# Recurrence of one layer: decays of the four-position level from products of gates in place of exponentials of sums

## The chip, the cores and the metric

The kernel runs on one core of one Trainium2 chip. The time is the device time of one execution of the whole program in microseconds (us), and the number compared is the median of several executions.

## What is computed

Four layers over 256 positions of width 1024, in float32. Each layer has a token mixer (layers 0 and 3: forgetting attention; layer 1: the HGRN2 recurrence; layer 2: a short convolution) and a mixture of experts, each behind a residual and a layer norm. The change touches layer 1's mixer alone:

```python
def hgrn2(x, w_in, lower_bound, norm_g, w_out):
    q, f_logit, i, g = jnp.split(x @ w_in, ...)
    f = lower_bound + (1.0 - lower_bound) * jax.nn.sigmoid(f_logit)
    log_f = jnp.log(f)
    k = 1.0 - f
    # per chunk, 8 heads of 128 key channels and 128 value channels
    b = jnp.cumsum(gb, axis=-2)
    diff = b[:, :, :, None, :] - b[:, :, None, :, :]
    decay = jnp.exp(jnp.where(causal[:, :, None], diff, -jnp.inf))
    scores = jnp.einsum('bhtk,bhsk,bhtsk->bhts', qb, kb, decay)
    o = jnp.einsum('bhts,bhsv->bhtv', scores, ib) + ...
```

Between a key at position s and a query at position t lies the product of the gates f at s+1 to t, for each of 128 channels.

## The kernel before, in words

**Levels.** The kernel does not form the decay of every pair. It cuts the 128 positions of a half of the tokens (c = 0, 1) into blocks of 2m for m = 64, 32, 16, 8, 4, 2, 1 (`LEVELS`). In a block of level m every key of the first half is multiplied by the gates between it and the block's middle, every query of the second half by the gates from the middle on, and the product of the two gives the scores of all pairs whose smallest common block this is. The tile `qk[:, h % 2, c, level, :]` holds these decayed keys and queries of a head, in two copies by turns. The level CROSS goes from the first 128 positions to the second.

**How the decays of a level are made.** Levels 64 to 4 (`SUMMED = 5` of them) and CROSS are exponentials of sums: PE multiplies the logs of the gates (`fg`, tokens on partitions) by tables of zeros and ones (`spans`), which gives the sums in PSUM (L958, L961 to L963), ScalarE drains three banks with `Exp` into `qk` (L1365 and L1367, in the profile as the helper's line L1220), and then DVE multiplies the query halves (L1758, one instruction a level, and L1760 for CROSS) and GpSimd (POOL) the key halves (L719, L721). Levels 2 and 1 (`TWO`, `ONE`) need no exponential: they are products of one or two gates with q or k, by DVE (L1750, L1751, L1753) and POOL (L713, L714), from `fT`, the gates with channels on partitions.

**A head on each engine.** The loop runs over h = 0 to 9, and in turn h each engine issues, in this order:

- PE: the sums of head h (L958 twice, L961, L962, L963); then for head h-1, behind a wait for DVE's `qd_ready` and POOL's `kd_ready`, the cross scores (L971), and for each half of the tokens three products of 128 columns (L978: levels 8, 4 and 2), one of 64 (L979: level 1) and seven small ones (L984: levels 64 to 16) into one bank; the diagonal (L992); then for head h-2 scores times values (L1005 to L1007). A matmul in float32 shows as two records in the profile.
- ScalarE: the three `Exp` drains of head h, the drain of the cross scores, the squares for the norm (L1379).
- DVE: for head h first L1750, L1751, L1753 (behind `sc` of head h-2), then, when all three drains of h are done, five L1758 and L1760. For head h-1 it picks the scores out of the banks (L1769, three L1773, L1780), for h-2 it gates the result (L1788).
- POOL: L713, L714, then behind the same drains five L719 and L721.

Ahead of the loop PE forms the projections of g and i from seven products of blocks each (L816); DVE makes sums of weights for them (L1606 to L1615) and joins the products (L1628, L1630). Behind the loop come the norm of the heads on POOL (L660) and DVE, transposes (L750), the output projection (L844), and, from the event `oT` on, the loads of expert weights into the five buffers that the recurrence's tiles had occupied.

```python
pe.wait_ge(qd_ready, g + 1)
pe.wait_ge(kd_ready, g + 1)
...
elif KINDS[l] == 1:
...
    sp.wait_ge(*filled(("oT", l, TC - 1, 1)))
```

## Time and profile before

| | us |
|---|---|
| median of 3 runs | 1454.54 (1454.23 to 1456.63) |
| the profiled execution | 1453.64 |
| its span, first to last instruction | 1451.8 |
| PE busy | 1307.7 (90%) |
| DVE busy | 365.1 (25%) |
| ScalarE busy | 305.7 (21%) |
| POOL busy | 96.5 (7%) |
| mean granted clock of PE | 0.988 |

Durations in the profile are those of the one profiled execution. A busy PE is one whose records, with modelled ends, leave no gap; the chain that ended last is followed back from the last instruction to what released each step. Times of day in the text, such as 484.78, are us from the start of the span.

### The profile page before, as it was taken

To read this page: it belongs to the slowest core of one execution; us is meant where nothing else is said; L and a number is where in the kernel's file an instruction comes from. 1 tells how busy PE (TensorE), PEld (TensorE's weight loads), DVE (VectorE), ACT (ScalarE), POOL (GpSimd) and SP (SyncE) were. 2 spreads that over 40 slices of the span, in tenths; PEclk is the share of its full clock that TensorE was granted. 3 is DMA by queue.
4 is the path that set the end of the run, shared out by engine and by line. 5 is a ranking of instruction groups with operands and counts; after the bars stand their busy time and mean duration, and the time that the engine had idled before them with its cause. 6 is when DMAs were issued, how large, how long until landed. Compare 5 with 4: busy or idle time off the path is not lost.

```text
span 1451.8 us, 18373 instructions
## 1 busy us (share of the span) xinstructions
PE 1307.7 (90%) x7662; PEld 735.0 (51%) x7662; DVE 365.1 (25%) x928; ACT 305.7 (21%) x751; POOL 96.5 (7%) x170
## 2 busy tenths in 40 slices
PE   8999988878999999898789999888789999988875
PEld 7855634332564766333328865343328765533421
DVE  1442311102624844101002033111112451311103
ACT  0231322211322322212112002222111251222210
POOL 2221000000000520000000000000001130000000
PEclk9999999999999999999999999999999999999998
DMA  9656699999835019999999937999998355899995
GB/s 327 262 226 285 236 430 427 428 426 415 337 116 206 28 56 421 428 428 427 428 425 366 398 117 277 429 427 426 430 423 364 139 232 232 324 427 427 427 427 228
DMA packets 36773, 481.97 MB, mean 332 GB/s; under 512 B 4416, under 2 KB 4736, under 8 KB 6864
## 3 DMA queue, kind: packets, MB, share of 16 engines
q1 hardware_dynamic: 35424, 478.19, 79.8%
q0 software_dynamic: 1120, 2.09, 0.7%
q8 instruction: 66, 1.08, 0.3%
q10 hardware_dynamic: 144, 0.46, 0.1%
q14 instruction: 19, 0.16, 0.0%
HBM read 479.60 MB, written 1.05 MB: 331 GB/s over the span
## 4 chain that ended last, share of the span: by engine, by line
PE 75%; DMA 13%; DVE 5%; ACT 4%; issue 2%; SPq 0%; POOL 0%; DVEq 0%; POOLq 0%
PE psum L785 15%; DMA memory<-in_units 13%; PE psum L1085 12%; PE psum L816 8%; PE psum L1045 8%; PE psum L844 8%; PE psum L1128 7%; PE psum L1120 7%; ACT memory L1224 2%; PE psum L824 1%; DVE memory L1912 1%; PE psum L750 1%; PE psum L1181 1%; ACT memory L1420 1%; PE psum L917 1%
## 5 line engine op out<-in xcount | busy, mean ns | idle before, releaser
L785 PE MATMUL psum<-memory,ring 128*128 128x256 f32 x1024 | 224.7, 382 | 0.4 <-ACT memory L1224 0.4
L785 PEld LDWEIGHTS psum<-memory,ring 128*128 128x128 f32 x1024 | 195.7, 192 | 28.6 <-issue 1.3
L1128 PE MATMUL psum<-memory 128*128 128x512 f32 x256 | 126.5, 619 | 42.9 <-DVE memory L1912 22.8
L1045 PE MATMUL psum<-memory,x 128*128 128x128 f32 x1024 | 131.0, 281 | 35.0 <-ACT memory L1224 35.0
L1045 PEld LDWEIGHTS psum<-memory,x 128*128 128x128 f32 x1024 | 119.8, 192 | 73.1 <-issue 70.2
L1085 PE MATMUL psum<-ring,memory 128*32 128x512 f32 x1152 | 135.9, 611 | 14.1 <-DMA ring<-in_units 13.9
L1224 ACT ACTIVATE memory<-psum,affine_t 128x128 f32<-128x128 f32 x312 | 117.3, 457 | 137.4 <-PE psum L1045 129.8
L1907 DVE TENSOR_TENSOR memory<-memory,psum 128x256 f32<-128x256 f32 x32 | 13.5, 421 | 459.4 <-ACT memory L1414 459.4
L844 PE MATMUL psum<-ring,memory 128*128 128x512 f32 x256 | 112.4, 594 | 1.4 <-DVE memory L1501 0.9
L1128 PEld LDWEIGHTS psum<-memory 128*128 128x128 f32 x256 | 44.0, 190 | 130.7 <-DVE memory L1912 48.2
L1085 PE MATMUL psum<-memory 128*32 128x512 f32 x896 | 103.0, 600 | 4.0 <-DMA memory<-in_units 3.9
L1220 ACT ACTIVATE memory<-psum 128x512 f32<-128x512 f32 (+2 forms) x85 | 45.5, 544 | 203.3 <-PE psum L816 103.4
L1085 PEld LDWEIGHTS psum<-ring,memory 128*32 128x32 f32 x1152 | 35.2, 112 | 104.2 <-issue 87.2
L816 PE MATMUL psum<-ring,memory 128*128 128x512 f32 x200 | 87.8, 593 | 0.0
L1120 PE MATMUL psum<-memory 128*32 128x512 f32 x640 | 79.6, 610 | 7.4 <-DMA memory<-in_units 7.4
L844 PEld LDWEIGHTS psum<-ring,memory 128*128 128x128 f32 x256 | 47.6, 190 | 57.1 <-issue 54.9
L1414 ACT ACTIVATE memory<-psum 128x256 f32<-128x256 f32 x32 | 12.3, 383 | 304.4 <-PE psum L1085 304.4
L1085 PEld LDWEIGHTS psum<-memory 128*32 128x32 f32 x896 | 26.6, 110 | 74.2 <-issue 68.9
L816 PEld LDWEIGHTS psum<-ring,memory 128*128 128x128 f32 x200 | 37.7, 190 | 45.5 <-issue 44.9
L1912 DVE COPY memory<-psum 128x512 f32<-128x512 f32 x32 | 22.1, 692 | 139.0 <-PE psum L1120 139.0
L1420 ACT ACTIVATE memory<-psum 128x512 f32<-128x512 f32 x32 | 19.1, 597 | 179.7 <-PE psum L1120 179.7
L1120 PE MATMUL psum<-ring,memory 128*32 128x512 f32 x384 | 48.8, 627 | 6.4 <-DMA ring<-in_units 6.4
(222 smaller groups left out, 1149.6 us busy)
## 6 DMA issues: line engine op xcount, KB each, us to landing
ring<-in_units SPq DMA_DIRECT2D x129, 2048.0 KB, 25.3
memory<-in_units SPq DMA_DIRECT2D x88, 2048.0 KB, 25.6
memory<-in_units SPq DMA_DIRECT2D x16, 1024.0 KB, 27.3
ring<-in_units SPq DMA_DIRECT2D x4, 512.0 KB, 10.4
memory<-in_const SPq DMA_DIRECT2D x3, 448.0 KB, 31.3
x<-in_x SPq DMA_DIRECT2D x2, 512.0 KB, 4.0
out<-x SPq DMA_DIRECT2D x2, 512.0 KB, 2.7
memory<-in_tables SPq DMA_DIRECT2D x1, 640.0 KB, 31.0
```

The costliest lines, as they stand in the source:

```text
L750: last = nc.tensor.transpose(bank(key, P, i * P), t, ident)
L785: last = nc.tensor.matmul(bank(key, T, s * T), w[:, 2 * m + s, k, :], xT[:, k, :], start=(k == 0), stop=(k == KD - 1))
L816: last = nc.tensor.matmul(bank(key), tokens[:, k, :], weights[:, k, :], start=(k == 0 and p not in (6, 7, 3)), stop=(k == KD // 2 - 1), sk ...
L844: last = nc.tensor.matmul(psum[:, 4 + NH * c + h, :], lhs[:, k, c * P:(c + 1) * P], w[:, k, :], start=False, stop=(k == KD - 1), skip_grou ...
L1045: last = nc.tensor.matmul(psum[:, to, (at + i) * P:(at + i + 1) * P], x[:, c, k * P:(k + 1) * P], sel[:, par, c, :], start=(c == 0), stop= ...
L1085: last = nc.tensor.matmul(psum[rows, 0, :].rearrange("p (t f) -> p t f", t=2), xw[:, k, rows], w[:, e, kk], start=(k == 0), stop=(k == KD ...
L1120: last = nc.tensor.matmul(psum[rows, 2 + h, :], hT[:, j, rows], w[:, e, j], start=(j == 0), stop=(j == FC - 1))
L1128: last = nc.tensor.matmul(psum[:, 4 + NH * c + h, :], hT[:, FC + c, :], y_sb[:, h * HB:(h + 1) * HB], start=False, stop=last_quad, skip_gr ...
L1220: nc.scalar.activation(dst, src, func, **kw).then_inc(drained_by["A"], 1)
L1224: return nc.scalar.activation(dst, src, ACT.Identity, scale=affine_t[:, j, 0, k:k + 1], bias=affine_t[:, j, 1, k:k + 1])
L1420: nc.scalar.activation(y_sb[:, HB:D], psum[:, 3, :], ACT.Copy).then_inc(sems["y1_ready"], 1)
L1912: v.tensor_copy(y_sb[:, 0:HB], psum[:, 2, :]).then_inc(sems["y0_ready"], 1)
```

## The change

Level 4 is no longer summed: `SUMMED` is 4, and a new level `FOUR` stands in its place in `qk`. The tables of sums lose 128 columns. In a block of eight positions the keys 0 and 1 take level TWO's keys 0 and 1 times f2·f3, the keys 2 and 3 are k times f3 and 1; the queries 4 and 5 are q times f4 and f4·f5, the queries 6 and 7 take level TWO's queries 6 and 7 times f4·f5. The factors are three tables over all heads (`g45`, `g3`, `g23`), made once by DVE with five instructions between two of its steps for the projection of g. In the loop DVE and POOL get two products a head each, POOL also a wait for its own copy, and lose one level product each; ScalarE's third drain has 256 columns instead of 512.

```diff
--- before.py
+++ after.py
@@ -96,8 +96,8 @@
 DIRECT = 3
 
 
-SUMMED = 5
-CROSS, TWO, ONE, NL = SUMMED, SUMMED + 1, SUMMED + 2, SUMMED + 3
+SUMMED = 4
+CROSS, FOUR, TWO, ONE, NL = SUMMED, SUMMED + 1, SUMMED + 2, SUMMED + 3, SUMMED + 4
 NM = len(LEVELS) - DIRECT
 
 
@@ -349,6 +349,10 @@
 
         fox_parts = region(work, EARLY_AT + (EARLY - 2) * UNIT, [2, KD // 2, HB])
         hgrn_sums = region(extra, 7168, [4, KD // 2, P])
+
+        g45 = region(extra, 9216, [HH, T // 8, 2])
+        g3 = region(extra, 9728, [HH, T // 8, 2])
+        g23 = region(extra, 10240, [HH, T // 8])
         hgrn_parts = region(extra, 0, [2, KD // 2, HB])
 
 
@@ -447,6 +451,7 @@
         ssqe_ready, rms_seed = sem("ssqe_ready"), sem("rms_seed")
         on_soon, pool_step = sem("on_soon"), sem("pool_step")
         odd_ready, level_picked = sem("odd_ready"), sem("level_picked")
+        products_made, two_ready = sem("products_made"), sem("two_ready")
 
         pad_set, y_conv = sem("pad_set"), sem("y_conv")
 
@@ -711,7 +716,16 @@
 
                             pool.wait_ge(*filled(("sc", l, h - 2, TC - 1)))
                         nc.gpsimd.tensor_tensor(e[:, :, :, 0], fours(k)[:, :, :, 0], fours(f)[:, :, :, 1], ALU.mult)
-                        nc.gpsimd.tensor_copy(e[:, :, :, 1], fours(k)[:, :, :, 1])
+                        step(nc.gpsimd.tensor_copy(e[:, :, :, 1], fours(k)[:, :, :, 1]))
+                        if h == 0:
+
+                            pool.wait_ge(products_made, 4)
+                        eights = lambda t: t.rearrange("p c (b r) -> p c b r", r=8)
+                        two, four = eights(qk[:, h % 2, :, TWO, :]), eights(qk[:, h % 2, :, FOUR, :])
+                        by = g23[:, h].rearrange("p (c b) -> p c b", c=TC).unsqueeze(3).to_broadcast([P, TC, P // 8, 2])
+                        nc.gpsimd.tensor_tensor(four[:, :, :, 0:2], two[:, :, :, 0:2], by, ALU.mult)
+                        nc.gpsimd.tensor_tensor(four[:, :, :, 2:4], eights(k)[:, :, :, 2:4],
+                                                g3[:, h].rearrange("p (c b) r -> p c b r", c=TC), ALU.mult)
                         pool.wait_ge(*drained(("E", l, h, 2)))
                         for i, m in enumerate(LEVELS[:SUMMED]):
                             e = qk[:, h % 2, :, i, :].rearrange("p c (b s m) -> p c b s m", s=2, m=m)[:, :, :, 0, :]
@@ -958,9 +972,8 @@
                             nc.tensor.matmul(bank(key), lfh[c], spans[:, 0:HB], start=True, stop=True).then_inc(bank_filled, 1)
                         key = ("E", l, h, 2)
                         free(key)
-                        nc.tensor.matmul(bank(key, 2 * P), lfh[0], spans[:, HB:HB + 2 * P], start=True, stop=True)
-                        nc.tensor.matmul(bank(key, P, 2 * P), lfh[1], spans[:, HB:HB + P], start=True, stop=True)
-                        nc.tensor.matmul(bank(key, P, 3 * P), lfh[1], tri, start=True, stop=True).then_inc(bank_filled, 1)
+                        nc.tensor.matmul(bank(key, P), lfh[0], spans[:, HB:HB + P], start=True, stop=True)
+                        nc.tensor.matmul(bank(key, P, P), lfh[1], tri, start=True, stop=True).then_inc(bank_filled, 1)
                     if 1 <= h <= HH:
                         g = h - 1
 
@@ -973,7 +986,7 @@
                         for c in range(TC):
                             key = ("sc", l, g, c)
                             free(key)
-                            for at, i in enumerate((DIRECT, DIRECT + 1, TWO)):
+                            for at, i in enumerate((DIRECT, FOUR, TWO)):
                                 kk = qk[:, g % 2, c, i, :]
                                 nc.tensor.matmul(bank(key, P, at * P), kk, kk, start=True, stop=True)
                             nc.tensor.matmul(bank(key, P, 3 * P)[:, 1::2], kT[:, g, c * P:(c + 1) * P], qk[:, g % 2, c, ONE, 1::2],
@@ -1364,7 +1377,7 @@
                             key = ("E", l, h, c)
                             drain(key, qk[:, h % 2, c, 0:4, :], bank(key).rearrange("p (i t) -> p i t", i=4), ACT.Exp)
                         key = ("E", l, h, 2)
-                        drain(key, qk[:, h % 2, :, 4:6, :], bank(key).rearrange("p (c i t) -> p c i t", c=TC, i=2), ACT.Exp)
+                        drain(key, qk[:, h % 2, :, CROSS, :], bank(key, T).rearrange("p (c t) -> p c t", c=TC), ACT.Exp)
                     if 1 <= h <= HH:
                         drain(("X", l, h - 1), scT[:, (h - 1) % 2, 2, :], bank(("X", l, h - 1), P))
                     if h == HH:
@@ -1726,6 +1739,15 @@
                 weight_sums(l, 4, "g", hgrn_parts, (1, 2, 3))
                 joined("g", l, sg_sb, [2])
                 weight_sums(l, 4, "g", hgrn_parts, (4,))
+                for c in range(TC):
+                    for half in range(2):
+                        dve.wait_ge(*drained(("kT", l, c, half)))
+                gate = fT.rearrange("p h (b r) -> p h b r", r=8)
+                v.tensor_copy(g45[:, :, :, 0], gate[:, :, :, 4])
+                v.tensor_tensor(g45[:, :, :, 1], gate[:, :, :, 4], gate[:, :, :, 5], ALU.mult).then_inc(products_made, 1)
+                v.tensor_copy(g3[:, :, :, 0], gate[:, :, :, 3]).then_inc(products_made, 1)
+                v.memset(g3[:, :, :, 1], 1.0).then_inc(products_made, 1)
+                v.tensor_tensor(g23, gate[:, :, :, 2], gate[:, :, :, 3], ALU.mult).then_inc(products_made, 1)
                 joined("g", l, sg_sb, (4, 3))
 
                 weight_sums(l, 6, "i", hgrn_parts, (1, 2, 3))
@@ -1750,7 +1772,16 @@
                         v.tensor_tensor(one[:, :, 1::2], q[:, :, 1::2], f[:, :, 1::2], ALU.mult).then_inc(odd_ready, 1)
                         v.tensor_tensor(fours(two)[:, :, :, 2], fours(q)[:, :, :, 2], fours(f)[:, :, :, 2], ALU.mult)
                         dve.wait_ge(odd_ready, h + 1)
-                        v.tensor_tensor(fours(two)[:, :, :, 3], fours(one)[:, :, :, 3], fours(f)[:, :, :, 2], ALU.mult)
+                        v.tensor_tensor(fours(two)[:, :, :, 3], fours(one)[:, :, :, 3], fours(f)[:, :, :, 2], ALU.mult).then_inc(two_ready, 1)
+                        if h == 0:
+
+                            dve.wait_ge(products_made, 4)
+                        eights = lambda t: t.rearrange("p c (b r) -> p c b r", r=8)
+                        four, by = qk[:, h % 2, :, FOUR, :], g45[:, h].rearrange("p (c b) r -> p c b r", c=TC)
+                        v.tensor_tensor(eights(four)[:, :, :, 4:6], eights(q)[:, :, :, 4:6], by, ALU.mult)
+                        dve.wait_ge(two_ready, h + 1)
+                        v.tensor_tensor(eights(four)[:, :, :, 6:8], eights(two)[:, :, :, 6:8],
+                                        by[:, :, :, 1:2].to_broadcast([P, TC, P // 8, 2]), ALU.mult)
                         dve.wait_ge(*drained(("E", l, h, 2)))
                         for i, m in enumerate(LEVELS[:SUMMED]):
                             e = qk[:, h % 2, :, i, :].rearrange("p c (b s m) -> p c b s m", s=2, m=m)[:, :, :, 1, :]
```

In the order of each engine, as it stands in the two programs (of numbers in a shape the first is the partitions; "waits" names the semaphores ahead of an instruction). First PE, in a middle turn, from scores times values of one turn to the cross scores of the next; before:

```order
L1007 MATMUL psum<-memory 128x128
L958 MATMUL psum<-memory 128x512 [waits drained_act] x2
L961 MATMUL psum<-memory 128x256 [waits drained_act]
L962 MATMUL psum<-memory 128x128
L963 MATMUL psum<-memory 128x128
L971 MATMUL psum<-memory 128x128 [waits drained_act,kd_ready,qd_ready]
```

and of the change:

```order
L1020 MATMUL psum<-memory 128x128
L972 MATMUL psum<-memory 128x512 [waits drained_act] x2
L975 MATMUL psum<-memory 128x128 [waits drained_act]
L976 MATMUL psum<-memory 128x128
L984 MATMUL psum<-memory 128x128 [waits drained_act,kd_ready,qd_ready]
```

L961 has half its columns as L975, L963 is L976, and L962 is gone.

DVE at the first head, from the join of the projection of i to the first instruction of head 1; before:

```order
L1630 TENSOR_TENSOR memory<-memory,psum 128x512 [waits bank_filled,drained_act]
L1750 TENSOR_TENSOR memory<-memory 128x2x64 [waits spans_in,sg_ready]
L1751 TENSOR_TENSOR memory<-memory 128x2x32
L1753 TENSOR_TENSOR memory<-memory 128x2x32 [waits odd_ready]
L1758 TENSOR_TENSOR memory<-memory 128x2x64 [waits drained_act]
L1758 TENSOR_TENSOR memory<-memory 128x2x2x32
L1758 TENSOR_TENSOR memory<-memory 128x2x4x16
L1758 TENSOR_TENSOR memory<-memory 128x2x8x8
L1758 TENSOR_TENSOR memory<-memory 128x2x16x4
L1760 TENSOR_TENSOR memory<-memory 128x128
L1750 TENSOR_TENSOR memory<-memory 128x2x64
```

and of the change:

```order
L1643 TENSOR_TENSOR memory<-memory,psum 128x512 [waits bank_filled,drained_act]
L1772 TENSOR_TENSOR memory<-memory 128x2x64 [waits spans_in,sg_ready]
L1773 TENSOR_TENSOR memory<-memory 128x2x32
L1775 TENSOR_TENSOR memory<-memory 128x2x32 [waits odd_ready]
L1781 TENSOR_TENSOR memory<-memory 128x2x16x2 [waits products_made]
L1783 TENSOR_TENSOR memory<-memory 128x2x16x2 [waits two_ready]
L1789 TENSOR_TENSOR memory<-memory 128x2x64 [waits drained_act]
L1789 TENSOR_TENSOR memory<-memory 128x2x2x32
L1789 TENSOR_TENSOR memory<-memory 128x2x4x16
L1789 TENSOR_TENSOR memory<-memory 128x2x8x8
L1791 TENSOR_TENSOR memory<-memory 128x128
L1772 TENSOR_TENSOR memory<-memory 128x2x64
```

The two products stand ahead of the wait for ScalarE, and the last of the five level products behind it is gone.

POOL at the first head, from its first product to the cross level's; before:

```order
L714 COPY memory<-memory 128x2x32
L719 TENSOR_TENSOR memory<-memory 128x2x64 [waits drained_act]
L719 TENSOR_TENSOR memory<-memory 128x2x2x32
L719 TENSOR_TENSOR memory<-memory 128x2x4x16
L719 TENSOR_TENSOR memory<-memory 128x2x8x8
L719 TENSOR_TENSOR memory<-memory 128x2x16x4
L721 TENSOR_TENSOR memory<-memory 128x128
```

and of the change:

```order
L719 COPY memory<-memory 128x2x32
L726 TENSOR_TENSOR memory<-memory 128x2x16x2 [waits products_made,pool_step]
L727 TENSOR_TENSOR memory<-memory 128x2x16x2
L733 TENSOR_TENSOR memory<-memory 128x2x64 [waits drained_act]
L733 TENSOR_TENSOR memory<-memory 128x2x2x32
L733 TENSOR_TENSOR memory<-memory 128x2x4x16
L733 TENSOR_TENSOR memory<-memory 128x2x8x8
L735 TENSOR_TENSOR memory<-memory 128x128
```

The same on POOL: two small products ahead of the wait, one level product less behind it.

## Rows read from the trace of the kernel before

**Rows 1.** The page, parts 1 and 5: engines in the whole span, a ScalarE group
```profile
PE 1307.7 (90%) x7662; PEld 735.0 (51%) x7662; DVE 365.1 (25%) x928; ACT 305.7 (21%) x751; POOL 96.5 (7%) x170
...
L1414 ACT ACTIVATE memory<-psum 128x256 f32<-128x256 f32 x32 | 12.3, 383 | 304.4 <-PE psum L1085 304.4
```

**Rows 2.** Stretches: us, PE, PEld, DVE, ACT, POOL busy (x), clock, DMA share, GB/s
```profile
480.00:520.00 40.00, 40.00 (x395) 32.94 (x394) 32.32 (x87) 14.16 (x46) 20.40 (x46) 1.00 0.01 2
560.00:600.00 40.00, 35.88 (x264) 22.01 (x266) 13.59 (x55) 11.37 (x27) 0.00 (x0) 1.00 1.01 421
...
484.62:491.59 6.97, 6.97 (x68) 5.63 (x67) 5.60 (x16) 2.58 (x8) 3.50 (x8) 1.00 0.00 0
```

**Rows 3.** Chain that ended last, one head: start us, us, what
```profile
484.78 1.72 PE psum L958 x4
486.50 0.43 PE psum L961 x2
486.93 0.22 PE psum L962 x2
487.15 0.22 PE psum L963 x2
...
491.76 1.72 PE psum L958 x4
```

**Rows 4.** Chain that ended last, first head of the recurrence
```profile
469.30 0.43 PE psum L961 x2
...
473.46 0.40 issue
```

**Rows 5.** PE in order of time, L971 of heads 0 and 1: [idle before]
```profile
473.86 0.46 PE L971 MATMUL psum<-memory 128*128 128x128 f32 x2 [1.09 <-DVE memory L1760]
...
480.24 0.39 PE L971 MATMUL psum<-memory 128*128 128x128 f32 x2
```

**Rows 6.** ACT in order of time, first head
```profile
469.34 0.60 ACT L1220 ACTIVATE memory<-psum 128x512 f32<-128x512 f32 x1 [0.52 <-PE psum L958]
470.21 0.60 ACT L1220 ACTIVATE memory<-psum 128x512 f32<-128x512 f32 x1 [0.28 <-PE psum L963]
```

**Rows 7.** POOL in order of time, first head
```profile
470.89 2.41 POOL L719 TENSOR_TENSOR memory<-memory 128x128 f32<-128x128 f32 x5 [6.16 <-ACT memory L1220]
473.26 0.50 POOL L721 TENSOR_TENSOR memory<-memory 128x128 f32<-128x128 f32 x1
```

**Rows 8.** DVE in order of time, first two heads
```profile
468.42 0.27 DVE L1753 TENSOR_TENSOR memory<-memory 128x64 f32<-128x64 f32 x1
470.84 2.14 DVE L1758 TENSOR_TENSOR memory<-memory 128x128 f32<-128x128 f32 x5 [2.15 <-ACT memory L1220]
...
473.83 0.50 DVE L1751 TENSOR_TENSOR memory<-memory 128x64 f32<-128x64 f32 x1
...
477.33 0.41 DVE L1769 TENSOR_TENSOR memory<-psum,memory 128x256 f32<-128x256 f32 x1
477.78 1.47 DVE L1773 COPY_PREDICATED memory<-memory,psum 128x256 f32<-128x256 int32 x3
```

**Rows 9.** DVE in order of time, a head in the middle
```profile
486.61 0.27 DVE L1753 TENSOR_TENSOR memory<-memory 128x64 f32<-128x64 f32 x1
488.04 2.15 DVE L1758 TENSOR_TENSOR memory<-memory 128x128 f32<-128x128 f32 x5 [1.17 <-ACT memory L1220]
```

**Rows 10.** POOL in order of time, the same head
```profile
488.09 2.41 POOL L719 TENSOR_TENSOR memory<-memory 128x128 f32<-128x128 f32 x5 [3.47 <-ACT memory L1220]
...
490.93 0.43 POOL L713 TENSOR_TENSOR memory<-memory 128x64 f32<-128x64 f32 x1
```

**Rows 11.** DVE in order of time, ahead of the recurrence
```profile
426.84 2.29 DVE L1615 TENSOR_TENSOR ring<-ring,memory 128x2048 f32<-128x2048 f32 x1
440.52 0.69 DVE L1628 TENSOR_TENSOR memory<-memory 128x512 f32<-128x512 f32 x1 [11.40 <-ACT memory L1220]
```

**Rows 12.** SyncE's queue, first load issued behind the recurrence
```profile
538.03 2.48 SPq L531 DMA_DIRECT2D memory<-in_units  x5
```

## The prediction

> **What bounds the kernel now.** I read the page first: TensorE (PE) is busy for 90% of the span [rows 1]. Then the busy times by stretch, because the change touches only the recurrence of layer 1, from about 467 to 530 us. In the forty microseconds from 480 PE is busy for all 40.00, VectorE (DVE) for 32.32, ScalarE for 14.16, GpSimd (POOL) for 20.40, with the granted clock at 1.00 (the level of 2.4 GHz) and the DMA engines at 0.01 [rows 2]. One head there takes 6.97 us, of which PE works 6.97, DVE 5.60, POOL 3.50 and ScalarE 2.58 [rows 2]. The chain that ended last says the same: from 484.78 to 491.76 it runs from one PE line into the next and through no other engine [rows 3]. So a head costs what PE does in it, and the head's levels, made by DVE and POOL, are waited for in one place only: at the first head, where PE stands idle for 1.09 us before L971 [rows 5]. The chain puts that on DVE's L1760 with 0.40 us of "issue" behind it [rows 4], but L971 waits for two engines, and POOL's L721 starts at 473.26 and takes 0.50, so it ends at 473.76, 0.10 before L971 starts at 473.86 [rows 7]. POOL is the late one.
>
> **PE's part.** The change takes one of six blocks of columns per half of the tokens out of the sums of decays: L961 shrinks from 256 columns to 128 and L962's 128 go. In the chain L961 takes 0.43 for its 256 columns, L962 and L963 0.22 each for 128 [rows 3]: 0.87 us before, 2 x 0.22 = 0.44 after, a saving of 0.43 us per head. The products of keys and queries keep their number and size: of the three 128-column ones the middle one only reads another level. Nothing is added to PE.
>
> **The first head.** Here there is more to gain, since PE waits. L961 starts at 469.30 [rows 4]; with 0.44 us of work instead of 0.87 the last bank is full at about 469.75. ScalarE is then still at the drain that starts at 469.34 and takes 0.60 [rows 6]; I let the next start at 469.81. It has 256 columns instead of 512, and the row nearest to it takes 0.383 us [rows 1] against 0.60 [rows 6], so it ends near 470.19 where it ended at 470.81: 0.62 us earlier. POOL then runs four level products instead of five, 2.41 / 5 = 0.48 us each [rows 7]. So the keys are ready 0.62 + 0.48 = 1.10 us earlier, and L971 starts at about 472.76. PE has by then done two heads' worth of less work, 0.87 us, so it arrives at 471.90 and still waits 0.86. The first two heads' sums together give 1.10.
>
> **The other heads.** Six more heads, 0.43 each: 2.6 us, if nothing else becomes late. Sum for the stage: 1.10 + 2.60 = **3.7 us**.
>
> **What covers the added work.** DVE: a head loses one of five L1758, 2.15 / 5 = 0.43, and gets two products of 64 elements a partition. The nearest row is L1753, also 64 elements and strided: 0.27 [rows 9]; the dearest of that size is L1751 at 473.83, 0.50, beside POOL at work [rows 8]. DVE was idle 1.17 of 6.97 [rows 9], so 5.80 becomes 5.80 - 0.43 + 0.54 = 5.91, at the dear end 6.37. Both are under the new 6.54. I take 0.27, because in the middle of the recurrence POOL has finished when DVE gets to its products: POOL's L713 is at 490.93 [rows 10], the products stand at 486.61 and a head later at 493.6. POOL: minus 0.48, plus two products of 64 elements (L713: 0.43 [rows 10]) and a wait for its own copy: 3.50 becomes 3.9, and they go into the 3.47 us in which it waits for ScalarE [rows 10]. Queued behind them are the level products, and behind those PE's L971; from the ends of both engines' level products to PE's use there are some 3.6 us in a middle head (DVE starts its five at 488.04 [rows 9] and is done 2.6 later; PE comes to the L971 that needs them two heads behind 480.24, at 494.2 [rows 5]).
>
> The tables (five instructions over 256 elements, L1746 to L1750 of the changed file): nearest is L1769, 256 elements, 0.41 [rows 8], so 2.1 us; at the price of the 512-element L1628, 0.69 [rows 11], 3.5 us. They stand behind L1615, which starts at 426.84 and takes 2.29, and ahead of L1628, before which DVE idles 11.40 us [rows 11]. Both ends fit. DVE's added wait for the copies of the gates is past long before. The added work at the first head stands before waits too: DVE idles 2.15 us ahead of its first L1758, POOL 6.16 [rows 7, 8]. The table load from memory is a tenth smaller and nothing waits for it; I cost it at nothing.
>
> **What happens to the gain behind the stage.** The next loads of expert weights are issued at 538.03 [rows 12], when PE has transposed the last heads' result; the DMA engines have been nearly empty since 480 and are full at 1.01 from 560 [rows 2]. Loads that start on an event behind the recurrence start 3.7 us earlier, and what hangs on them moves as a whole. Below, nothing is given back; above, nothing is won.
>
> Sum against the profiled execution: its span 1451.8 and 1453.64 with what lies around it; less 3.7 is 1449.9. The median of the runs shown lies 0.9 above it, 1454.54; the forecast for the median is 1454.54 - 3.7 = **1450.8 us**.
>
> **The rivals.**
>
> *The two engines get in each other's way.* Rows show it: L1751 takes 0.50 at 473.83, beside POOL, and its like 0.27 in the middle, without [rows 8, 9]. The place is the passage from head 0 to head 1, where DVE runs 15 instructions without a wait (from 470.84 to 477.33 [rows 8]) and POOL 14. Both numbers stay: two level products go on each engine, the two new products of head 1 come. Before, L1773 frees the banks of the scores at 479.25, and PE comes to fill them at about 480.46, 0.22 behind L971 at 480.24 [rows 5, 8]. After, PE comes 1.10 + 0.43 = 1.53 earlier, at 478.93, and DVE only 0.62, at 478.63: 0.3 us are left. If the new ones cost 0.50 instead of 0.27 on both engines and block each other, 0.2 to 0.9 us come on top, and PE waits up to 0.6. The time would be 1451.1 to 1451.4. The Trainium skill (SBUF — State Buffer, section Who interferes with whom) says that a DVE instruction with two SBUF inputs contends with a GpSimd instruction that reads SBUF, the second one blocked until the first is done. By that rule the trace's 0.50 against 0.27 is such a block, and the new products, with two SBUF inputs on either side, are all of this kind; it makes this rival's time, not the forecast's.
>
> *DVE becomes the bound, in part.* It does once its path, 5.37 without the new products, exceeds 6.54, so when one of them costs over 0.58. No row of 64 elements does (0.27 to 0.50). At 0.7 each, 6.77, the six heads gain 0.2 each instead of 0.43: 1.10 + 1.20 = 2.3 saved, 1452.2.
>
> *Slower than before: the same mechanism further on.* From 0.80 per product the head's path passes 6.97. At 1.2 (over twice the dearest row, if pieces of two elements at a stride of eight are handled badly) it is 7.77: 7 x 0.80 = 5.6 lost, 1.1 won, so 1459.0. Against it: L1753 already steps by four and costs 0.27.
>
> *The gain does not arrive.* If the expert stage behind it were held by something that does not start with the recurrence's end, the time would stay at 1454.5. Against it stands 0.01 of DMA during the stage [rows 2] and the one event that restarts it [rows 12].
>
> **How the numbers follow.** Forecast 0.70 (1450.1 to 1451.6 with the spread of medians), engines in each other's way 0.13, DVE partly the bound 0.08, gain not arriving 0.05, slower 0.04. The three runs shown differ by 2.4 us and their median by 0.9 from the profiled one, so about 0.2%, 2.9 us, is what a measurement of this kernel tells from no change. The forecast lies 0.8 beyond that. Faster: 0.70 of the first case less a tenth, and nearly all of the second, 0.76; within 0.2%: 0.20; slower: 0.04. The range takes in the first two cases, most of the third and about a microsecond of spread of the medians on either side: 1449.3 to 1453.0.
>
> **What would show it.** In the profile after: a middle head of 6.54 us with PE busy throughout; the line that answers to L971 (L984 of the changed file) at the first head near 472.8, with under 0.9 us of idle time; DVE's two new products near 0.27 each and its wait for ScalarE still there; POOL's wait for ScalarE near 2.2; the tables inside the 11.4 us; the load behind the recurrence issued at about 534.3. The prediction is wrong if PE's rows show idle time in the middle heads, if the sums of a head do not shrink by 0.43, or if the load moves and the end does not.

## The result, and the profile after

The change made the kernel slower: median 1468.18 us (1462.96 to 1469.53, 7 runs) against 1454.54 (1452.25 to 1459.95, 7 runs) of the kernel before on the same chip, a ratio of 1.0076 [1.0057, 1.0095]. The forecast was 1450.8, in a range of 1449.3 to 1453.0. The profiled execution took 1469.53, its span is 1467.5, 15.7 us more than before; its mean clock is 0.986.

The page of the changed kernel, parts 1 and 3, against [rows 1]: PE has 16 records fewer, and yet 1.3 us more of busy time. The second line is the same in both kernels: 66 packets of instructions, 1.08 MB, so 16.4 KB a packet (16,384 bytes each by the trace's own list of packets).

```profile
PE 1309.0 (89%) x7646; PEld 736.4 (50%) x7646; DVE 367.0 (25%) x941; ACT 303.5 (21%) x751; POOL 98.0 (7%) x178
...
q8 instruction: 66, 1.08, 0.3%
```

**The stage that was changed did what was forecast.** Stretches of the recurrence, columns as in [rows 2]: a head takes 6.54 us, PE is busy in all of them, DVE 5.50, POOL 3.65.

```profile
480.00:520.00 40.00, 40.00 (x411) 32.93 (x411) 32.24 (x92) 12.79 (x49) 22.43 (x55) 1.00 0.01 2
482.63:489.17 6.54, 6.54 (x65) 5.24 (x65) 5.50 (x17) 2.27 (x8) 3.65 (x10) 1.00 0.00 0
```

The chain that ended last, one head ahead of that of [rows 3]: the two sums of the third bank take 0.22 each, and the next head begins 6.55 after this one.

```profile
476.08 1.72 PE psum L972 x4
477.80 0.22 PE psum L975 x2
478.02 0.22 PE psum L976 x2
...
482.63 1.72 PE psum L972 x4
```

PE at the first head, beside [rows 5]: L984 waits 0.89 us.

```profile
472.14 0.46 PE L984 MATMUL psum<-memory 128*128 128x128 f32 x2 [0.89 <-DVE memory L1791]
```

DVE in order of time: the five instructions for the tables, then its two new products at the passage from head 0 to head 1, with POOL at work, then the same two in a middle head and what follows them.

```profile
428.38 0.39 DVE L1746 COPY memory<-memory 128x256 f32<-128x256 f32 x1
428.68 0.62 DVE L1747 TENSOR_TENSOR memory<-memory 128x256 f32<-128x256 f32 x1
429.21 0.40 DVE L1748 COPY memory<-memory 128x256 f32<-128x256 f32 x1
429.61 0.27 DVE L1749 MEMSET memory<- 128x256 f32 x1
429.79 0.49 DVE L1750 TENSOR_TENSOR memory<-memory 128x256 f32<-128x256 f32 x1
...
472.82 0.21 DVE L1781 TENSOR_TENSOR memory<-memory 128x64 f32<-128x64 f32 x1
472.95 0.32 DVE L1783 TENSOR_TENSOR memory<-memory 128x64 f32<-128x64 f32 x1
...
484.61 0.21 DVE L1781 TENSOR_TENSOR memory<-memory 128x64 f32<-128x64 f32 x1
484.75 0.22 DVE L1783 TENSOR_TENSOR memory<-memory 128x64 f32<-128x64 f32 x1
485.29 1.68 DVE L1789 TENSOR_TENSOR memory<-memory 128x128 f32<-128x128 f32 x4 [0.32 <-ACT memory L1233]
```

POOL, the same middle head, beside [rows 10]:

```profile
485.33 1.95 POOL L733 TENSOR_TENSOR memory<-memory 128x128 f32<-128x128 f32 x4 [2.56 <-ACT memory L1233]
```

SyncE's queue, the load behind the recurrence, beside [rows 12]:

```profile
533.73 2.59 SPq L536 DMA_DIRECT2D memory<-in_units  x5
```

From the first sum of head 0 to the norm of the heads on POOL the stage took 55.25 us before (467.16 to 522.41) and takes 51.60 now (466.50 to 518.10): 3.65 us less, where the sum said 3.7.

**The time came in elsewhere, in code that the change does not touch.** Behind the experts of each layer stands a branch, in the program of PE, ScalarE, DVE and SyncE (`more_path`): a body for tokens that overflow the experts' slots, which is jumped over here. PE's call of it is L1213; behind it come three fill-in matmuls of 512 columns (L758, six records), which keep PE busy while the sums of the norm are made, and then the transposes of the next layer (L764).

```python
with eng.If(over > 0):
    body(l, runs)
```

The chain that ended last, of the changed kernel, around this branch in layer 1 and in layer 2:

```profile
755.85 3.63 PE psum L1141 x8
759.48 4.68 issue
764.16 4.51 PE psum L758 x6
768.67 1.75 PE psum L764 x16
...
1087.80 3.63 PE psum L1141 x8
1091.43 4.42 issue
1095.85 4.46 PE psum L758 x6
```

PE in order of time at the same two places of the kernel before (L1128 there is L1141 here, L744 is L758, L750 is L764):

```profile
760.06 3.70 PE L1128 MATMUL psum<-memory 128*128 128x512 f32 x8
763.60 2.75 PE L744 MATMUL psum<-const 128*128 128x512 f32 x6
766.91 1.26 PE L750 MATMUL psum<-const,x 128*128 128x128 f32 x9 [0.56 <-ACT x L1271]
...
1083.27 3.70 PE L1128 MATMUL psum<-memory 128*128 128x512 f32 x8
1086.81 2.75 PE L744 MATMUL psum<-const 128*128 128x512 f32 x6
1090.12 2.02 PE L750 MATMUL psum<-const,x 128*128 128x128 f32 x16 [0.56 <-ACT x L1271]
```

Before, the fill-in follows on the experts' last product without a gap. After, PE stands 4.68 and 4.42 us with "issue" as the reason: it waits for nothing that the profile shows. Both layers' fill-in then takes 4.5 us instead of 2.75. The windows show the clock beside it (changed kernel first, then the kernel before): behind the 4.68 and 4.42 us of idle time PE's clock is granted at 0.69 and 0.66, so for much of these stretches at its lower level of 1.2 GHz, and once more later, 0.83 over twenty microseconds in layer 3's projection, with PE busy throughout.

```profile
765.00:770.00 5.00, 5.00 (x19) 2.63 (x19) 0.41 (x2) 0.85 (x3) 0.79 (x2) 0.69 1.04 416
1095.00:1100.00 5.00, 4.15 (x6) 1.84 (x7) 0.72 (x2) 0.19 (x1) 3.50 (x1) 0.66 0.98 389
1120.00:1140.00 20.00, 20.00 (x94) 17.59 (x94) 3.76 (x2) 1.79 (x4) 3.50 (x1) 0.83 0.46 175
```

```profile
765.00:770.00 5.00, 4.40 (x25) 2.94 (x24) 4.69 (x17) 4.34 (x11) 1.02 (x2) 1.00 1.00 377
1085.00:1090.00 5.00, 4.56 (x11) 1.70 (x9) 4.29 (x14) 2.12 (x7) 0.43 (x1) 1.00 0.99 366
1120.00:1140.00 20.00, 20.00 (x110) 18.03 (x109) 13.32 (x10) 7.99 (x13) 3.51 (x1) 1.00 0.37 121
```

Divided at the same instructions of the two profiled executions, the 15.7 us are these:

| stretch | before, us | after, us | difference |
|---|---|---|---|
| start to the last product of layer 1's experts (L1128, L1141) | 760.06 | 755.78 | -4.28 |
| from there over the branch to the transposes | 6.85 | 12.73 | +5.88 |
| layer 2, to the last product of its experts | 316.36 | 319.22 | +2.86 |
| over the branch to the transposes | 6.85 | 12.41 | +5.56 |
| layer 3's mixer, to its router | 150.65 | 153.94 | +3.29 |
| to the end | 211.03 | 213.42 | +2.39 |

The two branches cost 11.4. The 3.29 have the size of the clock's dip there: twenty microseconds at 0.83 are 3.4 lost. The 2.86 and the 2.39 lie in stages that are full of DMA and vary from run to run, as the experiments show.

### The profile page after: what moved, and what is told of

Same layout as the page of the kernel before. It is cut to its first block, busy times and chain, and to the rows that moved or that the text cites. A ratio compares the mean times of both kernels' runs of the same rounds, so it can differ in the third digit from the quotient of the medians.

```text
span 1467.5 us, 18365 instructions
## 1 busy us (share of the span) xinstructions
PE 1309.0 (89%) x7646; PEld 736.4 (50%) x7646; DVE 367.0 (25%) x941; ACT 303.5 (21%) x751; POOL 98.0 (7%) x178
## 3 DMA queue, kind: packets, MB, share of 16 engines
q8 instruction: 66, 1.08, 0.3%
## 4 chain that ended last, share of the span: by engine, by line
PE 76%; DMA 13%; DVE 4%; ACT 3%; issue 2%; SPq 0%; POOL 0%; DVEq 0%; POOLq 0%
PE psum L799 15%; DMA memory<-in_units 13%; PE psum L1098 12%; PE psum L830 8%; PE psum L1058 8%; PE psum L858 8%; PE psum L1141 7%; PE psum L1133 7%; ACT memory L1237 2%; PE psum L838 1%; DVE memory L1943 1%; PE psum L1194 1%; ACT memory L1433 1%; PE psum L931 1%; PE psum L758 1%
## 5 line engine op out<-in xcount | busy, mean ns | idle before, releaser
L1141 PE MATMUL psum<-memory 128*128 128x512 f32 x256 | 127.6, 624 | 42.9 <-DVE memory L1943 22.8
L1098 PE MATMUL psum<-ring,memory 128*32 128x512 f32 x1152 | 132.9, 600 | 15.7 <-DMA ring<-in_units 15.6
L1141 PEld LDWEIGHTS psum<-memory 128*128 128x128 f32 x256 | 44.3, 192 | 131.5 <-DVE memory L1943 48.2
L1233 ACT ACTIVATE memory<-psum 128x512 f32<-128x512 f32 (+3 forms) x85 | 42.9, 524 | 204.1 <-PE psum L830 106.4
L758 PE MATMUL psum<-const 128*128 128x512 f32 x90 | 47.6, 652 | 9.1 <-issue 9.1
```

The costliest lines, as they stand in the source:

```text
L758: nc.tensor.matmul(psum[:, bank_no, :], ident, ident.unsqueeze(1).to_broadcast([P, HB // P, P]), start=True, stop=True)
L1098: last = nc.tensor.matmul(psum[rows, 0, :].rearrange("p (t f) -> p t f", t=2), xw[:, k, rows], w[:, e, kk], start=(k == 0), stop=(k == KD ...
L1141: last = nc.tensor.matmul(psum[:, 4 + NH * c + h, :], hT[:, FC + c, :], y_sb[:, h * HB:(h + 1) * HB], start=False, stop=last_quad, skip_gr ...
L1233: nc.scalar.activation(dst, src, func, **kw).then_inc(drained_by["A"], 1)
```

## The experiments

The theory after the first look (A): the change takes eight matmuls out of PE's instructions, and so moves all code behind them; what matters is where in memory the code behind the branch comes to lie. The rivals: the wait comes because the expert loads start earlier, by 4.3 us in the profiled executions (538.03 to 533.73) (B), or it is a cost of the change's own (C). In the text of the later runs, D is the sharpened form of A: what counts is the place in a block of 256 instructions, so 64 matmuls. E is its rival: what counts is the distance from a fixed place, or the time, and the pattern doesn't come back after a block.

**e1, the change with as many matmuls as before.** The third bank's first sum goes in two halves, in each of eight heads.

```diff
-                        nc.tensor.matmul(bank(key, P), lfh[0], spans[:, HB:HB + P], start=True, stop=True)
+                        for half in range(2):
+                            nc.tensor.matmul(bank(key, P // 2, half * P // 2), lfh[0], spans[:, HB + half * P // 2:HB + (half + 1) * P // 2], start=True, stop=True)
```

> The change, with the sum over 128 columns of the first half of the tokens issued as two of 64: same columns and same work, but PE has as many instructions in the recurrence as before the change. Theory A (the place of PE's code behind the recurrence has moved by eight matmuls, and PE waits for its code at the two branches behind the experts of layers 1 and 2, 4.68 and 4.42 us): both waits of the kind 'issue' are gone, PE goes from the last expert product into the filling matmuls without a gap as before the change, and the time is 4 us below before, near 1450.5. Theory B (the 4 us earlier start of the weight loads makes the code or the small loads come at a worse moment): the waits stay, since the recurrence is as short as in the change, and the time stays near 1467.

PE behind layer 1's branch, in order of time: no wait, and none in layer 2.

```profile
762.44 2.75 PE L758 MATMUL psum<-const 128*128 128x512 f32 x6
```

The median is 1455.57 (10 runs) against 1457.48 (20 runs) on the same chip, ratio 0.9992 [0.9976, 1.0009]. The expected 4 us below before did not come, and the interval contains 1, so no change. The stage took 53.12, so 2.1 less than before and 1.5 more than the change: the halves are dear, which explains a part of the miss. The waits are gone with the change's mathematics, loads and early start in place.

**e2, the kernel before with eight matmuls fewer.** L962 and L963 are one matmul of 256 columns; the queries' cross sum is thereby another one than the reference's.

```diff
-                        nc.tensor.matmul(bank(key, P, 2 * P), lfh[1], spans[:, HB:HB + P], start=True, stop=True)
-                        nc.tensor.matmul(bank(key, P, 3 * P), lfh[1], tri, start=True, stop=True).then_inc(bank_filled, 1)
+                        nc.tensor.matmul(bank(key, 2 * P, 2 * P), lfh[1], spans[:, HB:HB + 2 * P], start=True, stop=True).then_inc(bank_filled, 1)
```

> The kernel before, with L962 and L963 merged into one matmul of 256 columns (the sum for the cross level of the queries is another one, so the output of the cross level is wrong): same columns and time of the recurrence as before, eight matmuls fewer in PE's code. Theory A: the waits 'issue' of over 4 us appear at the branches behind the experts of layers 1 and 2, with the recurrence at its old length, and the time is some 14 to 18 us above before. Theory B: no such wait, time within 1 us of before.

1468.82 (4 runs), ratio 1.0079 [1.0056, 1.0103]: the whole loss, without anything of the change. PE waits 4.41 and 5.20 us behind the two branches. That is 11.3 us above before, under the expected 14 to 18. The stage took 55.14, as before, so no load is earlier for its sake, and the programs of DVE, ScalarE and POOL are those of the kernel before. B and C fall with e1 and e2 together.

**e3, eight matmuls added between the two branches.** One block of layer 2's projection goes in halves of 128 columns (the sums of this block are not the reference's). The line shown stands around the matmul, which then takes the columns of `part`.

```diff
+                            for part in ([slice(0, P), slice(P, T)] if (l, name, m0 + m, s) == (2, "b", 3, 1) else [slice(0, T)]):
```

> The change, with eight matmuls of 256 columns of layer 2's first projection split in two of 128, behind the first of the two branches and ahead of the second: no added columns, PE's code is as long as before the change only from there on. Theory A: the wait of 4.7 us at the branch behind layer 1 stays, the one behind layer 2 goes; time between before and the change, about 1457 to 1461. Theory B: both stay, time as the change.

PE behind the two branches:

```profile
767.85 4.51 PE L758 MATMUL psum<-const 128*128 128x512 f32 x6 [3.90 <-issue]
...
1094.07 2.75 PE L758 MATMUL psum<-const 128*128 128x512 f32 x6
```

The first branch, ahead of which eight are missing, has its wait of 3.90; the second, ahead of which none are, has none. 1462.34 (8 runs), ratio 1.0033 [1.0014, 1.0053], between the others and 1.3 above the top of what was expected. So what counts is the number of PE instructions ahead of each branch.

**e4, half of it.** e1's halves in heads 0 to 3 only, so four matmuls fewer than before. The edit is shown against e1; in the other heads the matmul keeps its 128 columns.

```diff
-                        for half in range(2):
+                        for half in ((0, 1) if h < 4 else (0,)):
```

> The change, with the split of the first kernel of this call in heads 0 to 3 alone: PE's code behind the recurrence is displaced by four matmuls instead of eight. Theory A: at each of the two branches the wait is either there, of a similar size, or not, depending on where the code lies: it tells whether half the displacement is enough, and whether the wait grows with it (half of 4.7 us) or is all or nothing. Theory B: as the change.

4.33 and 4.16 us of wait; 1468.02 (3 runs), ratio 1.0077 [1.0048, 1.0105]. Four fewer are as bad as eight fewer.

**e5, the change with eight tiny matmuls.** They stand in layer 1's router, behind fill-in matmuls and ahead of a wait for DVE, into a bank that nobody reads.

```diff
                 keep_busy(2, FILLS.bank["xT", 2 * l, 1, 0])
+                for _ in range(8 if l == 1 else 0):
+                    nc.tensor.matmul(psum[0:16, FILLS.bank["xT", 2 * l, 1, 0], 0:16], ident[:, 0:16], ident[:, 0:16], start=True, stop=True)
```

> The change, with eight matmuls of 16 columns into a bank that is not read, behind the two filling matmuls of layer 1's router, where PE waits 0.8 us for DVE: PE's code is from there on as long as before the change, and the recurrence keeps its short sums. Theory A (place of PE's code): no wait of the kind 'issue' at the branches behind the experts of layers 1 and 2, the recurrence 3.6 us shorter as in the change, time 3 to 4 us under before. Theory C (the sums, the products on DVE and POOL, or the earlier loads cost something of their own behind the recurrence): at or above before in spite of the waits being gone.

PE at the router, then at the two branches:

```profile
568.22 0.56 PE L1202 MATMUL psum<-const 128*16 128x16 f32 x16
569.12 0.38 PE L1207 MATMUL psum<-memory 128*128 128x32 f32 x2 [0.33 <-DVE memory L1898]
...
757.47 3.70 PE L1141 MATMUL psum<-memory 128*128 128x512 f32 x8
761.00 2.75 PE L758 MATMUL psum<-const 128*128 128x512 f32 x6
...
1088.56 2.75 PE L758 MATMUL psum<-const 128*128 128x512 f32 x6
```

The sixteen records take 0.56 us, and L1207 behind them still waits 0.33 for DVE, where its like in the changed kernel (L1205) waits 0.83: they cost nothing. No wait at the branches, the fill-in takes 2.75. The median is 1454.23 (11 runs) against 1457.54 (15 runs), ratio 0.9978 [0.9969, 0.9987]: this version is faster than the kernel before by 3.3 us, which agrees with what the stage gains, 3.65. Against the changed kernel's own ratio of 1.0076 the eight tiny matmuls are worth 1.0%, some 14 us.

**e6 to e12, where the edges are.** The same edit with other numbers: 7, 12, 40, 72, 71, 64 and 6 tiny matmuls in place of 8, the first of them shown against e5.

```diff
-                for _ in range(8 if l == 1 else 0):
+                for _ in range(7 if l == 1 else 0):
```

Single runs: what is compared is the wait, not the time.

> The same with seven matmuls instead of eight: PE's code is displaced by one matmul against before. Theory A: the waits are there or not at each branch; the value tells how near the edge the kernel before stood. With the half displacement both waits were there, so the edge lies between no and four matmuls; even chance. Where a wait is there it is 4 to 5 us, not an eighth of it.

> The same with twelve: displaced by four matmuls to the other side of before. Theory A: again all or nothing at each branch; if the good place is a wide one, no wait, time as with eight.

> The same with forty: displaced by 32 matmuls, 128 instructions, to the other side, half of the 256 instructions (16 KB) that one packet of the instruction queue carries. Theory A: if the place within such a block decides, some displacement between none and a block brings the waits; at half a block even chance. The forty small matmuls themselves may cost up to 3 us, about 0.8 of it covered.

> The change with 72 of the small matmuls, 64 more than in the kernel that put the code back: 256 instructions, just what one packet of the instruction queue carries (16 KB). They take 0.027 us a record, so 3.9 us in all, 0.8 of it in PE's wait. Theory D (what decides is the place within such a block of 256): the same place as with 8, so no wait 'issue' at either branch, time about 3 us above the kernel with 8. Theory E (it is a matter of the distance from a fixed place, or of time): no reason for the pattern of 8 to come back.

> With 71: by theory D the same place as with 7, so the wait of over 4 us comes at the branch behind layer 2 and not at the one behind layer 1. By theory E both are absent or the pattern is another.

> With 64: by theory D the same place as with none, the change itself, so both waits come back, 4 to 5 us each, and the time is near 1470 in spite of the code being longer than in the kernel with 8. By theory E nothing brings them back.

> With 6: displaced by two matmuls against before. The wait at the branch behind layer 2 stays as with 7; at the one behind layer 1 the edge lies between one and four matmuls, so even chance. All or nothing: where the wait is there it is 4 to 5 us.

All runs, by the number of matmuls ahead of the branch against the kernel before. The times come from several chips and are to be read with care: beside e1 to e4 the kernel before had a median of 1457.48, beside e5 to e8 1457.54, and beside e9 to e12 it ran once, 1462.57.

| matmuls | run | wait in layer 1, us | in layer 2, us | time, us |
|---|---|---|---|---|
| -8 | the change | 4.68 | 4.42 | 1468.18 |
| -8 | e2 | 4.41 | 5.20 | 1468.82 |
| -4 | e4 | 4.33 | 4.16 | 1468.02 |
| -2 | e12 (6 tiny) | 4.76 | 4.65 | 1468.43 |
| -1 | e6 (7 tiny) | none | 4.33 | 1458.96 |
| 0 | before, e1, e5 | none | none | 1454.54, 1455.57, 1454.23 |
| +4 | e7 (12 tiny) | none | none | 1453.08 |
| +32 | e8 (40 tiny) | none | none | 1458.07 |
| +56 = 64 - 8 | e11 (64 tiny) | 4.79 | 4.25 | 1464.64 |
| +63 = 64 - 1 | e10 (71 tiny) | none | 1.26 | 1461.85 |
| +64 | e9 (72 tiny) | none | none | 1456.80 |
| -8, then 0 | e3 | 3.90 | none | 1462.34 |

PE behind the branches in e6, 7 tiny matmuls (layer 1, layer 2):

```profile
758.69 2.75 PE L758 MATMUL psum<-const 128*128 128x512 f32 x6
...
1089.72 4.51 PE L758 MATMUL psum<-const 128*128 128x512 f32 x6 [4.33 <-issue]
```

in e11, 64 of them (layer 1):

```profile
765.67 4.32 PE L758 MATMUL psum<-const 128*128 128x512 f32 x6 [4.79 <-issue]
```

in e10, 71 (layer 2):

```profile
1094.42 2.83 PE L758 MATMUL psum<-const 128*128 128x512 f32 x6 [1.26 <-issue]
```

and in e9, 72 (layer 1):

```profile
763.03 2.75 PE L758 MATMUL psum<-const 128*128 128x512 f32 x6
```

With 7 instead of 8 the wait comes back in layer 2 and not in layer 1, with 6 in both: layer 2's edge lies between 0 and -1, layer 1's between -1 and -2. So the kernel before can't lose even one matmul ahead of layer 2's branch without the wait. The other runs repeat the pattern 64 matmuls further on; in e10 the wait is there, but 1.26 us long instead of over 4, which the theory did not say: it is not all or nothing right at the edge. e11's single time, 1464.64, is 5 us under the expected 1470, with both waits at their full length. E falls: e11 lies 56 matmuls from the kernel before and waits, e9 lies 64 from it and doesn't.

## Why the prediction was wrong

- **The stage's sum held.** PE's part: the sums of the third bank went from 0.87 to 0.44, the heads from 6.97 to 6.54. The first head: L984 started at 472.14, 5.48 after the first sum of the recurrence (466.66) where L971 started 6.54 after it (473.86 against 467.32), so 1.06 for the forecast 1.10, with 0.89 us of idle time for 0.86. POOL is the late one again: its L735 ends at 472.04, DVE's L1791 at 471.72. In all 3.65 for 3.7.
- **What covers the added work held.** DVE's new products take 0.21 and 0.22 where 0.27 were taken, and its wait for ScalarE is still there, 0.32. That is half of the 0.63 that the sum left it; as much again, 0.52, it now waits for PE's L997, where it had no such wait before. POOL's wait is 2.56 for the forecast 2.2; the tables take 1.9 us, far inside DVE's idle time. The load behind the recurrence was issued at 533.73 (forecast 534.3).
- **The engines in each other's way** did not cost anything. Beside POOL the second new product takes 0.32 instead of 0.22, not 0.50, and PE came to head 1's scores without a wait. DVE's three old products of head 1, which run beside POOL as before, are the ones that are dearer there: 0.54, 0.49 and 0.38, against 0.28, 0.27 and 0.28 in the middle head. The first new one, 0.21, is not, though POOL's L726 starts (472.85) before it ends (473.03). The rule of the Trainium skill (SBUF — State Buffer, section Who interferes with whom), which I had given this rival's time, agrees with the trace in direction, and shows in the new products only as this 0.10.
- **DVE as the bound, in part or wholly,** fell with 0.21 a product; the time came out on its slower side, but by nothing that this rival names. "The gain does not arrive" is wrong as well: it arrived at 533.73 and still stood at 755.78, 4.28 us ahead of before.
- **The step that failed** is two sentences that I costed at nothing. The first, "Nothing is added to PE", is true of its work, but eight matmuls were taken from its code, and I followed only what they cost and not where the code behind them came to lie. The second is "what hangs on them moves as a whole. Below, nothing is given back": given back were 5.88 and 5.56 us at two branches, 230 and 560 us further on, and more through the clock. No row that I had read tells of this. The rows at the two branches of the kernel before show no wait, and that it stood one matmul from one can't be seen in them; what could be seen is that the program has branches on PE, and that the number of PE's instructions ahead of them changes.

**What the mechanism is, and how far it is shown.** Shown by the runs: the wait depends on the number of PE instructions ahead of the branch and on nothing else that was tried (e1 to e5), and the pattern comes back after 64 float32 matmuls. Such a matmul is two records of PE and two of PEld, so these are 256 instructions, and 64 bytes for each of 256 is one packet of instructions. By the waits alone a period of 16 or 32 matmuls would fit as well, for e8, 32 on, has none either.

The packets decide that. Queue 8 of the trace carries packets of 16,384 bytes only. Between the branches of layers 0 and 1 of the kernel before one of them starts every 255 records of PE and PEld on average, between those of layers 1 and 2 every 262. e11, which is the changed kernel with 64 matmuls more on PE and nothing else, has one packet more, and so have e9 and e10:

```profile
q8 instruction: 67, 1.10, 0.3%
```

So this queue brings PE its program, in pieces of 256 instructions. Around layer 1's branch a packet starts 0.34 us after the first record of the last product in e5 and 0.55 in e9, 64 matmuls on; in e8, 32 on, the nearest starts 5.1 after it. What the packets do at the branches of layers 1 and 2, in all fourteen traces:

| passages | the packet starts | PE goes on |
|---|---|---|
| 12 with a wait of 3.9 to 5.2 us | 1.0 to 2.3 us after the end of PE's last product | 2.6 to 3.0 us after that start |
| e10 in layer 2, a wait of 1.26 us | 1.4 us before that end | 2.7 us after that start |
| 13 without a wait | 3.0 to 6.7 us before the fill-in | at once |
| e8, both, without a wait | over 15 us before the fill-in, the next one after its start | at once |

In the changed kernel, for example, the packet starts at 761.24 and PE goes on at 764.16; in the kernel before it starts at 760.50, while PE still works. So no wait comes where the packet has started 3.0 us or more ahead of PE's need, and where it starts later PE goes on 2.6 to 3.0 us behind its start; e10's wait is short because its packet started early, and why it did is open. The Trainium skill (Runtime: NRT & Kernel Launch, section Instruction fetch mechanics) states that an engine's instructions come in blocks of 16 KiB, 256 instructions, that only what follows in sequence is fetched ahead, and that a taken branch whose target lies outside the present two pages makes the engine wait for a fetch. The runs here agree with the block in its size, and the packets at the waits agree with a fetch that comes too late for the jump. That it is the jump's target which is fetched, and that it lies outside the two pages in these runs and inside them in the others, is inferred: no trace shows addresses, or when a fetch was asked for. Layer 0's branch can't tell anything, since every run has the same 3839 records of PE and PEld ahead of its fill-in (no gap at 357 in either kernel).

**The clock adds to the price.** By rows: the two fill-ins took 4.51 and 4.46 instead of 2.75, 3.5 us together, beside 9.1 us of wait. The fill-in behind a full wait took 4.3 to 5.5 us wherever its row was read, and 2.75 behind none (2.83 behind e10's 1.26), so this part goes with the wait. The later dip, in layer 3's projection, goes with it less closely. From 1110 to 1145, with PE busy throughout, the granted clock is 0.90 in the changed kernel and 0.95 in the other six runs with a wait at layer 2's branch, but 0.95 in e7 too, which has no wait; in the six others it is 1.00. Here are the changed kernel, e7 and the kernel before:

```profile
1110.00:1145.00 35.00, 35.00 (x164) 30.77 (x163) 8.51 (x6) 6.67 (x11) 3.50 (x1) 0.90 0.47 180
...
1110.00:1145.00 35.00, 35.00 (x172) 30.95 (x171) 14.68 (x12) 7.99 (x13) 3.50 (x1) 0.95 0.40 150
...
1110.00:1145.00 35.00, 35.00 (x180) 31.23 (x179) 13.60 (x11) 7.99 (x13) 3.51 (x1) 1.00 0.55 215
```

Over the whole span the clock took only some 3 us more than before (an estimate: 0.014 of 1467.5 us against 0.012 of 1451.8), because the kernel before has dips that the changed one has not: for one, layer 0's last expert product takes 4.32 us before and 3.70 after.

**Open** are the 2.86 us in layer 2 and the 2.39 in the last experts. Between the two branches, from transposes to transposes, the runs with no wait at the second, or e10's short one, took 323.2 to 327.6 us, and e5, with the best of the medians, is over 327; so some 4 us of difference there come from something else than the place of the code. e8's forty matmuls take 2.17 us by their records, of which some 0.8 lie in PE's wait for DVE, and e8 is 3.8 above e5; a single run doesn't settle more. Whether any of this comes from the change was not tried.

## What to carry to other kernels

After any edit that changes the number of instructions of an engine that has a branch further on, look for gaps with "issue" right behind the branches, before and after, ahead of judging the edit: here they hid a gain of 3.65 us under a loss of 14. Where one is found, pad with matmuls as small as they go (0.03 us a record) inside a wait that is there anyway, and choose a number away from the edge (4 more than needed was as good in one run, 1 less was not). A saving is added up stage by stage, but an idle PE can cost more than its length: here the three fill-in matmuls behind a full wait took 1.6 to 2.7 us more, at the lower clock.

## What the runs showed of the hardware that was not expected

- One float32 matmul more or fewer, 568 us into the program and worth 0.07 us of PE, decides over a wait of 4.33 us at 1085 us (e6 against e5).
- Where the wait comes, PE stands 3.9 to 5.2 us behind a jump in twelve cases of thirteen, and goes on 2.6 to 3.0 us after the start of a packet of 16,384 bytes on the instruction queue. The loads of weights keep the DMA engines at 0.98 to 1.04 in these windows; whether the wait is that long because of those loads was not tried.
- DVE's products of 64 elements in pairs at a stride of eight (0.21) are cheaper than those of single elements at a stride of four (0.27). They differ in a second point too: one input of the former is a small table without gaps or a repeated value of it.
